# Moving four column-product tiles of a two-block transformer kernel into the waits before two norms, and two others inside the second layer

## The reference, cut to what matters

```
cs = silu(c)
for l in range(2):
    sh1, sc1, g1, sh2, sc2, g2 = split(cs @ ada_w[l] + ada_b[l], 6)
    x = x + g1 * mixer(rms_norm(x) * (1 + sc1) + sh1)
    x = x + g2 * moe(rms_norm(x) * (1 + sc2) + sh2)
x = rms_norm(x, final_g)
sh1, sc1, gt1, sh2, sc2, gt2 = split(silu(c_2) @ w_mod + b_mod, 6)
y = hybrid_mixer(layer_norm(x) * (1 + sc1) + sh1)
x = layer_norm(ALPHA * x + (1 + gt1) * y, ln1_g, ln1_b)
y = moe2(layer_norm(x) * (1 + sc2) + sh2)
x = layer_norm(ALPHA * x + (1 + gt2) * y, ln2_g, ln2_b)
```

## Time and profile before

| What | Value |
|---|---|
| median of 3 runs | 1316.29 us (1316.22, 1316.29, 1320.61) |
| the profiled execution, its own time | 1314.97 us |
| its span, first to last instruction | 1312.9 us |
| TensorE busy | 1211.2 us (92%) |
| VectorE, ScalarE, GpSimd busy | 496.1, 275.1, 113.8 us |
| mean granted TensorE clock | 0.97 of full |
| moved from HBM | 355 MB |

### The profile page before, as it was taken

How to read it: one execution, slowest core, us unless ns; L and a number is a source line. 1 busy time by engine, 2 the same in 40 slices (tenths; PEclk the granted TensorE clock), 3 DMA queues, 4 the chain that set the end, 5 groups by cost and what they waited for, 6 DMA issues and landing times.

```text
span 1312.9 us, 18617 instructions
## 1 busy us (share of the span) xinstructions
PE 1211.2 (92%) x7752; PEld 702.3 (53%) x7752; DVE 496.1 (38%) x1210; ACT 275.1 (21%) x651; POOL 113.8 (9%) x202
## 2 busy tenths in 40 slices
PE   4899989999799899899987999999999699999996
PEld 4788655434687665643446845655544443332333
DVE  1655542113764773411153643331132640201134
ACT  0113421212112462211122121113320211020110
POOL 2110010000111000100000000000000222122121
PEclk8999999999899899899998999999999799999999
DMA  9977949999946563599996333294325489999993
GB/s 354 386 215 244 386 149 356 387 387 387 338 137 218 200 227 138 197 383 387 387 386 243 136 128 122 73 388 143 105 100 209 174 315 409 393 387 397 386 386 148
DMA packets 173805, 357.46 MB, mean 272 GB/s; under 512 B 15845, under 2 KB 20502, under 8 KB 173718
## 3 DMA queue, kind: packets, MB, share of 16 engines
q1 hardware_dynamic: 171710, 353.14, 73.6%
q10 hardware_dynamic: 2008, 3.07, 0.7%
HBM read 355.14 MB, written 1.05 MB: 271 GB/s over the span
## 4 chain that ended last, share of the span: by engine, by line
PE 60%; DVE 5%; DMA 5%; ACT 3%; issue 1%; SPq 0%; POOL 0%; DVEq 0%; ACTq 0%
PE bank L2775 9%; PE bank L2285 7%; PE bank L3071 4%; PE bank L2424 4%; PE bank L2302 4%; PE bank L2549 4%; DMA ring<-in_w_down 3%; PE bank L3131 3%; PE bank L2349 2%; PE bank L2851 2%; PE bank L2598 2%; DMA ring<-in_moe_w_down 1%; PE bank L2519 1%; PE bank L2717 1%; PE bank L2416 1%
## 5 line engine op out<-in xcount | busy, mean ns | idle before, releaser
L2775 PE MATMUL bank<-ring,A 128*64 128x512 f32 x512 | 115.2, 597 | 1.7 <-DVE pb L1884 1.7
L2549 PE MATMUL bank<-ring,A 128*64 128x512 f32 x512 | 116.0, 598 | 0.0
L2285 PE MATMUL bank<-ring,OT 128*128 128x512 f32 x224 | 97.2, 593 | 1.3 <-ACT OT L1292 0.8
L2349 PE MATMUL bank<-ring,cact 128*32 128x128 f32 x2304 | 85.6, 305 | 9.9 <-DMA ring<-in_ada_w 7.5
L841 POOL TENSOR_TENSOR rstd<-rstd,nhalf 128x1 f32<-128x1 f32 x20 | 15.7, 787 | 796.6 <-DVE rstd L1416 796.5
L2349 PEld LDWEIGHTS bank<-ring,cact 128*32 128x32 f32 x2304 | 70.7, 123 | 24.0 <-issue 15.6
L2775 PEld LDWEIGHTS bank<-ring,A 128*64 128x64 f32 x512 | 34.8, 136 | 71.7 <-issue 70.8
L2285 PEld LDWEIGHTS bank<-ring,OT 128*128 128x128 f32 x224 | 42.2, 190 | 53.5 <-issue 52.5
L2549 PEld LDWEIGHTS bank<-ring,A 128*64 128x64 f32 x512 | 34.3, 136 | 65.3 <-issue 64.2
L2302 PE MATMUL bank<-ring,hT 128*128 128x256 f32 x264 | 62.6, 392 | 2.3 <-ACT hT L966 2.3
L2598 PE MATMUL bank<-ring,pb 128*64 128x512 f32 x256 | 57.7, 597 | 0.2
(11 more groups left out here) (503 smaller groups left out, 1895.4 us busy)
## 6 DMA issues: line engine op xcount, KB each, us to landing
ring<-in_ada_w SPq DMA_DIRECT2D x24, 2048.0 KB, 9.3
ring<-in_moe_w_gate SPq DMA_DIRECT2D x32, 1024.0 KB, 12.3
ring<-in_moe_w_up SPq DMA_DIRECT2D x32, 1024.0 KB, 14.2
ring<-in_moe_w_down SPq DMA_DIRECT2D x16, 2048.0 KB, 19.8
ring<-in_w_gate SPq DMA_DIRECT2D x16, 2048.0 KB, 11.2
ring<-in_w_up SPq DMA_DIRECT2D x16, 2048.0 KB, 11.2
ring<-in_w_down SPq DMA_DIRECT2D x16, 2048.0 KB, 20.4
ring<-in_w_in SPq DMA_DIRECT2D x13, 2048.0 KB, 19.6
```

What stands on the lines that cost most here:

```text
L2285: ins = mm(B[2 * (m % 2) + tt][:], lhs[:, c, tt * P:(tt + 1) * P], w[:, c, :], start=c == 0, stop=c == C - 1)
L2349: ins = mm(B[MOD_RAW_BANK[G]][32 * q:32 * (q + 1), k * P:(k + 1) * P], cact[:, c0 + c:c0 + c + 1].broadcast_to([P, 32]), w[:, c, q * P:(q ...
L2549: ins = mm(B[b][64 * odd:64 * (odd + 1), :], wide_h[c][:, slot:slot + 64], w[:, 2 * pair + odd, :, r, :], start=c == 0, stop=c == C - 1)
L2775: ins = mm(B[b][64 * odd:64 * (odd + 1), :], wide_h[c][:, slot:slot + 64], w[:, 2 * pair + odd, r, :], start=c == 0, stop=c == C - 1)
```

## The change

Six tiles get other places; all products stay the same, and no instruction of them is dropped.

1. Group 4's first two tiles are computed between layer 0's experts and the norm of h2. Its other two come between two groups of transposes and just before the compressed scores. Its turn is behind those scores, and VectorE's part behind the compressed softmax. ScalarE copies it in two halves (`mod_half_out`). Group 5 alone is left in the attention, over 20 of its 24 steps.
2. The old group 8 becomes group 7: two tiles between layer 1's experts and the norm of h4, turned behind the thin product of h4. The "gated" group becomes group 8.
3. TensorE reads the overflow flag earlier: before the last down-product instead of after the last scatter. A wait on `moe_added` is put into the block that is skipped.
4. The order of loads follows: each moved tile is loaded before the tiles that it overtakes.

The diff, cut to its core:

```diff
-          ("odin", 5), ("cmp", 2), ("mod_c", 8), ("odout", 2), ("mod_h4", 4), ("moe1", 24),
-          ("xbc", 4), ("z", 2), ("qkv", 3), ("mod_gated", 4), ("ssdo", 2), ("gates", 4), ("atto", 1),
-          ("wo", 1), ("mod_merged", 2), ("wo_last", 1), ("mod_last", 2), ("moe2", 48)]
+          ("mod_c", 2), ("odin", 5), ("cmp", 2), ("mod_c_rest", 6), ("odout", 2), ("mod_h4", 4), ("moe1", 24),
+          ("mod_merged", 2), ("xbc", 4), ("z", 2), ("qkv", 3), ("mod_gated", 4), ("ssdo", 2), ("gates", 4), ("atto", 1),
+          ("wo", 2), ("mod_last", 2), ("moe2", 48)]
...
-    MOD_WORK = {"att0": (1, (4, 4)), "att1": (4, (12, 12)), "att2": None}
+    MOD_WORK = {"att0": (1, (4, 4)), "att1": (5, (20,)), "att2": None}
...
@@ ScalarE
         trans_out("h2", modulated(1, 0))
+        tile_ready(act, mod_tile_of(4, 1))
+        a.copy(mod_raw(4)[:, 0:256], B[1][:, 0:256]).then_inc(s["mod_half_out"], 1)
...
         a.activation(kcmpT[:], B[6][:, 0:60], ACT.Identity, bias=b2k[:, 0:1]).then_inc(s["act_once"], 1)
+        tile_ready(act, mod_tile_of(4, 3))
+        a.copy(mod_raw(4)[:, 256:512], B[2][:, 256:512]).then_inc(s["mod_raw_out"], 1)
...
         small_act("moe1")
+        mod_out(7)
         trans_out("h4", modulated(2, 0))
...
@@ VectorE
-        attention("att1", compressed_softmax)
+        def beside_first():
+            compressed_softmax()
+            mod_columns(4)
+        attention("att1", beside_first)
...
         trans_out("h4", modulated(2, 0))
+        mod_columns(7)
...
         norm_end(xn, x, 0, True, power).then_inc(s["xn_ready"], 1)
-        mod_columns(8)
...
@@ TensorE
+                if (name, j) == ("odin", 1):
+                    pe.wait_ge(s["mod_half_out"], 1)
...
             for q in range(1, 4):
                 down(q, 0)
                 scatter(q - 1)
+                if q == 3:
+                    over = overflows(pe, name)
                 down(q, 1)
             scatter(3)
-            moe_rest_pe(name)
+            moe_rest_pe(name, over)
...
         small_experts("moe0")
+        for k in range(2):
+            mod_tile(4, k)
         pe.wait_ge(s["moe_added"], 1)
         token_transposes("h2", xn, "xn_ready", 4)
...
-        for g in range(8, 12):
+        for g in range(8, 10):
+            qkv_group(g)
+        mod_tile(4, 2)
+        for g in range(10, 12):
             qkv_group(g)
...
         ins.then_inc(s["vcmp_ready"], 1)
+        mod_tile(4, 3)
         pe.wait_ge(s["act_once"], ACT_ONCE["kcmp_out"])
...
         ins.then_inc(s["cscore_ready"], 1)
+        mod_turn(4)
         pe.wait_ge(s["cscore_out"], 1)
         attention("att1")
...
         small_experts("moe1")
+        for k in range(2):
+            mod_tile(7, k)
         pe.wait_ge(s["moe_added"], 2)
         token_transposes("h4", xn, "xn_ready", 8)
         thin_products(wdf, 24, "h4")
+        mod_turn(7)
...
-        project("wo", 1, OT)
-        for k in range(2):
-            mod_tile(8, k)
-        project("wo", 2, OT, 1)
-        mod_turn(8)
+        project("wo", 2, OT)
```

54 lines of the change are left out of this document (31 added, 23 removed).

## The result

The changed kernel takes **1325.99 us** (median of 4 runs, 1324.72 to 1327.0), the kernel before 1316.26 beside it (1316.01 to 1320.61): a ratio of 1.0059, 95% interval 1.0037 to 1.0081. A later series of ten runs gave 1325.88 us, 1.0049 (1.0024 to 1.0073). That is about 10 us slower, where 3.3 us less were forecast, and outside the range (1309.2 to 1317.2).

The account below looks back on a forecast made before the run. TensorE, busy 92% of the span, was taken as the bound; terms -3.6 + 0.3 - 1.0 - 1.1 + 1.5 + 0.6 = -3.3 us against the median 1316.29 gave 1313.0 us, range 1309.2 to 1317.2.

Parts of the forecast that it names:

- Before h2, cover: Before h2's norm: two mod tiles of 3.63 us fit the 5.0 us wait, 1.4 us to spare, cost 0.
- The tiles don't hide before h2: Rival, chance 0.16: branch and code fetch on TensorE outlast the 1.4 us to spare, 2 us delay; 1316.2 us.
- Before h2, clock: At h2's 16 transposes: the shorter wait keeps the clock up, 2.1 us instead of 3.65; -1.0 us, at worst 0.
- rule and trace: At h2's transposes: skill says transposes don't engage full rate, making the clock term 0; the trace speaks against it.
- Attention, -1.1: Second layer's attention: fewer mod pieces in the chain, pieces beside maxima and exponentials save nothing; -1.1 us, between -2 and 0.
- The clock takes it back: Rival, chance 0.12: the new order shifts clock falls and rises around h2, scores, h4 and last norm; +3.3, 1319.6 us.
- Between projection and attention, +1.5: Two tiles before the compressed scores add 2.15 us, clock gain takes off 0.6; +1.5 us, from +0.9 to +3.7.
- wholly at full clock: Case for the compressed scores: 4.1 us instead of 5.27 if the clock stays up throughout, -1.2 us.
- comes later: At the compressed scores: a later clock fall would hit the attention, so only half the gain, -0.6, was taken.
- Output projection, -3.6: Between the halves of wo: two mod tiles leave the chain, their 3.63 us go in full; -3.6 us.
- Before h4, +0.3: Before h4: two tiles hide in an 11.0 us wait; two transposes of the turn after the thin product cost +0.3 us.
- The flag, +0.6: TensorE's earlier flag read before the last down-product of both small experts: 0.3 us each, +0.6 us, 0 to 2.2.

Follow-up runs that it names:

- e4: Changed kernel with TensorE's part of the small experts' skipped block cut to a single wait: 1321.18 us, ratio 1.0011 to the kernel before.
- e9: The changed kernel itself, run again without any edit: 1325.88 us, ratio 1.0049 to the kernel before.
- e13: Changed kernel with group 5's chunks laid 1, 2, 2 in step with the attention's groups of three, same 20 steps: 1319.78 us, ratio 1.0002.
- e17: Changed kernel with group 5's chunks laid 1, 1, 2 over all 24 attention steps: 1314.29 us, ratio 0.9978 to the kernel before.
- e1: Changed kernel with group 4 put back as before, leaving the output projection's part and the earlier flag read: 1314.46 us, ratio 0.9974.
- e2: Changed kernel with the merged pair back between the halves of `wo`, group 4 still moved: 1328.88 us, ratio 1.0094 to the kernel before.
- e10: e1's kernel with three of every eight chunks of groups 4 and 5 left out in the second layer's attention: 1309.84 us, ratio 0.9929.
- e5: Changed kernel with the second layer's attention steps filled to the old number of parts by unused products on constants: 1324.08 us, ratio 1.0038.
- e8: Changed kernel with group 5's four tiles over the attention's first 12 steps in place of 20: 1321.11 us, ratio 1.0018.
- e18: e1's kernel run again: 1313.96 us, ratio 0.9973 to the kernel before.
- e16: Changed kernel with the skipped block cut to a single wait and group 5's chunks aligned as 1, 2, 2: 1313.34 us, ratio 0.9960.
- e14: e1's kernel with its attention steps thinned to the changed kernel's chunk numbers per step, output incomplete: 1317.11 us, ratio 1.0006.
- e15: Changed kernel computing only two of eight chunks of the two tiles between projection and attention: 1325.31 us, ratio 1.0054.

## Why the prediction was wrong

**Before h2, cover: wrong, and the first cause.** "1.4 us to spare" counted only the tiles. The step took the branch over the skipped block for 0.3 us, VectorE's price, because TensorE's own had always lain under the norm wait. It is 4.0 us. The rival "The tiles don't hide before h2" had this mechanism, with 2 us; it stopped at half the size, took the cold clock for a lost gain and not for a cost of the tiles, and put the whole case 3.2 us above the forecast. The stage lost 3.8 us. e4, without the stall, fell by 4.7.

**Before h2, clock: right in kind, void in the sum.** The transposes ran in 1.97 us instead of 3.65, so transposes don't keep the clock down, and rule and trace stay apart as told there. But the tiles paid for it in the cold (6.58 us against 3.63). Where the stall was absent (e4), the transposes ended 1.7 us sooner, more than the 1.0 forecast.

**Attention, -1.1: wrong, and the largest error, +10.8 in the profile.** (In e9, the second execution, it was +6.1, with 2.3 more ahead of it.) The working assumed that the clock stays at 1.00, as in the earlier trace rows. In warm groups its arithmetic holds: e13 and e17 take 8.7 us where 8.9 stood. What failed is that the clock's state was no term of this step at all. The rival "The clock takes it back" had the fall but dismissed it with "nothing in the new order adds rest anywhere". The mod parts beside VectorE's maxima, 0.86 us each, which the step called worth nothing because they are off the chain, are where most was taken: 27 of the 32 chunks that left, out of TensorE's rests, and the last four steps lost all of theirs. That taking them out costs is shown by e1 and e2; that it costs by how the rest is laid, and not by the amount, is shown by the times of e10 and e17 against the changed kernel, with e5 left unexplained. The Trainium skill describes a pattern of this kind (TensorE: Matmul & The Clock Gate, A second HAM failure mode: psum-queue depth-cycling): an engine that idles briefly and often between groups of matmuls is throttled and released again and again. The first profile agrees, one fall a group, 10.45 us against 8.88, with rests of at most 1.5 us; e9, the same program, shows it at both ends only.

**Between projection and attention, +1.5: right, as far as it can be told.** +0.4 in the first profile, under the step's range, and +2.3 in e9, inside it. The scores took 3.83 us, below even the 4.1 of "wholly at full clock": the rates of 22 and 13 count a record in both windows that it touches, and with the cold 3.0 us simply halved the step would have had 3.8. The fall that "comes later" did not cost the first steps: the granted clock of the first group was 0.88 against 0.64 before. It was the second group's that fell, to 0.84 from 1.00.

**Not in the sum at all:** the 2.1 us ahead of the second set of odin's products, where VectorE's sums are now waited for longer and the clock fell, in this execution and not in every one (0.4 us in e5, e8 and e17).

**Output projection, -3.6: right.** -3.4 together with the turn's +0.3; e18 has it as a ratio of 0.9973. **Before h4, +0.3: nearly right;** the stall costs nothing there. The 1.3 us of warm transposes were not in the step; they are a by-product of the stall. Stall and cold tiles fill the wait to its end, and in all nine executions with the stall at this place the transposes take 2.30 us; in the nine with tiles and without it TensorE rests some microseconds behind the tiles, and they take 3.37 to 3.65. **The flag, +0.6: 0.** It was taken between two bounds without a row, and the lower one holds (3.87 us before and after).

One reading of rows was off without any weight: the queue's rates in the earlier trace rows are 385 to 403 GB/s, not 384 to 389. Right terms, then, for the parts with a row, and a sum that failed on two quantities that the old trace couldn't show because something covered them: a stall under a wait, and a clock that work of no apparent worth helped to hold up.

What stays open: why the clock falls in one execution and not in another of the same program (82.7 and 87.4 us; e13's end and e16's), why e5 gained nothing, and where a long block stalls at the jump and where later. Shown as levers are the short block (e4), the parts laid over all 24 steps as in e17, by its time, and parts up to the last step, for the end. Alignment by itself has one time for it (e13, whose interval just meets that of the changed kernel). How the single dip comes about isn't shown.

## What to carry to other kernels

Work that is put into an engine's wait takes away the cover of everything else that hid in it: ask what ends there besides the wait, above all a jump over code, and put such work into a wait that is longer than both together (h4: 11 us) rather than one that just fits (h2: 5 us). Filler in a loop that waits on other engines isn't free to remove because it is off the chain. When some of it goes, carry the rest up to the loop's last step, and try it in step with the loop's period, which went with a gain in e13 and e17 and not in e5. And where the clock moves, one profile shows one of several outcomes: decide on ten runs, and use profiles to see what differs.

## What the hardware showed beyond that

- A jump over 80 matmuls with their weight loads cost TensorE 3.93 to 4.08 us in eighteen places with tiles right behind it; in three others (e10, e14 and e15 before h4) nothing at the jump and 1.5 to 2.7 us a little later. Over half as many: nothing at the jump, 1.5 us after 74 records in one layer, nothing in the other.
- The same code at nearly the same busy share (87 and 88%) ran at a granted clock of 0.84 or 1.00.
- Leaving out work made e10's attention 1.3 us shorter than e1's; laying the same work differently made e17 some 9 us faster than the changed kernel. The size of the effects doesn't follow the amounts of work.
- Sixteen transposes ran in 1.94 to 1.97 us at 2.4 GHz right behind tiles (h2 in the changed kernel and e4), and in 3.65 us at 1.2 GHz.
